# Seven block products for half of three output projections, in a two-stack transformer kernel on one core

## The reference

```python
def mamba2_mixer(h, in_w, conv_w, conv_b, dt_bias, a_log, d_skip, norm_w, out_w):
    ...
    y = y.reshape(bsz, seq, M_D_INNER).astype(h.dtype) * jax.nn.silu(z)
    gs = M_D_INNER // M_GROUPS
    y = rmsnorm_2(y.reshape(bsz, seq, M_GROUPS, gs), norm_w.reshape(M_GROUPS, gs))
    return y.reshape(bsz, seq, M_D_INNER) @ out_w

def gated_deltanet_mixer(h, in_w, conv_w, a_log, dt_bias, norm_w, out_w):
    ...
    o = rmsnorm_2(o.astype(h.dtype), norm_w) * jax.nn.silu(z.reshape(bsz, seq, G_V_HEADS, G_HEAD_DIM))
    return o.reshape(bsz, seq, G_VAL_DIM) @ out_w
```

## Time and profile before

| | before |
|---|---|
| median of three runs | 3557.66 us |
| profiled execution | 3557.7 us |
| its span, first to last instruction | 3556.0 us |
| TensorE busy | 3522.7 us, 99% |
| VectorE busy | 1956.5 us, 55% |
| ScalarE busy | 757.6 us, 21% |
| mean granted TensorE clock | 0.997 |

### The profile page before, as it was taken

The page is one execution under the profiler, slowest core; times in us unless marked ns, Lnnn a source line. Parts: engine busy times, 40 slices in busy tenths (PEclk is TensorE's granted clock), DMA queues, the critical chain, the costliest instruction groups (busy, mean ns, idle before and its releaser), DMA issues.

```text
span 3556.0 us, 47847 instructions
## 1 busy us (share of the span) xinstructions
PE 3522.7 (99%) x20724; PEld 2721.1 (77%) x20724; DVE 1956.5 (55%) x3405; ACT 757.6 (21%) x1504; POOL 52.6 (1%) x72
## 2 busy tenths in 40 slices
PE   8999999999999999999999999999999999999999
PEld 7956597794669687488868879687677968758794
DVE  6854378584535536236735648547443853635484
ACT  2003400100420045212113111042311103521110
POOL 1000000000000000000002000000000000000000
PEclk9999999999999999999999999999999999999999
DMA  9763468654325453334443434433143444334342
GB/s 414 305 263 139 169 257 330 271 208 166 119 108 190 166 190 119 130 142 160 173 166 119 179 119 167 166 140 121 72 159 127 166 166 176 147 127 151 139 166 107
DMA packets 45778, 613.32 MB, mean 172 GB/s; under 512 B 5040, under 2 KB 5056, under 8 KB 8960
## 3 DMA queue, kind: packets, MB, share of 16 engines
q1 hardware_dynamic: 41296, 590.99, 44.4%
q0 software_dynamic: 4272, 19.27, 1.4%
HBM read 607.02 MB, written 3.22 MB: 172 GB/s over the span
## 4 chain that ended last, share of the span: by engine, by line
PE 97%; ACT 1%; DVE 1%; issue 0%; DMA 0%; ACTq 0%
PE ps L3051 14%; PE ps L1513 13%; PE ps L588 9%; PE ps L481 8%; PE ps L705 7%; PE ps L567 5%; PE ps L2859 4%; PE ps L2378 4%; PE ps L2411 3%; PE ps L929 3%; PE ps L2951 3%; PE ps L1895 2%; PE ps L1915 2%; PE ps L1890 2%; PE ps L730 2%; PE ps L3245 1%
## 5 line engine op out<-in xcount | busy, mean ns | idle before, releaser
L588 PE MATMUL ps<-ring,aT 128*128 128x512 f32 x784 | 341.4, 592 | 0.0
L588 PEld LDWEIGHTS ps<-ring,aT 128*128 128x128 f32 x784 | 147.9, 190 | 179.1 <-issue 178.9
L705 PEld LDWEIGHTS ps<-hT,ring 128*128 128x128 f32 x2368 | 266.9, 192 | 5.7 <-issue 4.3
L705 PE MATMUL ps<-hT,ring 128*128 128x128 f32 x2368 | 268.4, 275 | 0.0
L567 PE MATMUL ps<-ring,aT 128*128 128x512 f32 x448 | 194.1, 592 | 0.0
L624 ACT ACTIVATE big<-x 128x1024 f32<-128x1024 f32 x34 | 35.9, 1057 | 695.2 <-DVE x L678 394.1
L2378 PE MATMUL ps<-hT,ring 128*128 128x256 f32 x768 | 173.4, 386 | 0.0
L567 PEld LDWEIGHTS ps<-ring,aT 128*128 128x128 f32 x448 | 84.5, 190 | 103.5 <-issue 103.3
L2378 PEld LDWEIGHTS ps<-hT,ring 128*128 128x128 f32 x768 | 147.7, 194 | 20.1
L3051 PE MATMUL ps<-big 128*128 128x128 f32 x1280 | 156.0, 275 | 0.0
L3051 PE MATMUL ps<-big,ring 128*128 128x128 f32 x1280 | 156.0, 275 | 0.0
(11 more groups left out here) (657 smaller groups left out, 6017.9 us busy)
## 6 DMA issues: line engine op xcount, KB each, us to landing
ring<-weights_in SPq DMA_DIRECT2D x244, 2048.0 KB, 7.8
big<-ada_in SPq DMA_DIRECT2D x36, 2048.0 KB, 9.1
aT<-rows_spill POOLq DMA_DIRECT2D x4, 1024.0 KB, 6.6
big<-rows_spill POOLq DMA_DIRECT2D x4, 1024.0 KB, 13.4
memT<-spill POOLq DMA_DIRECT2D x2, 1024.0 KB, 7.5
big<-b_gate_in POOLq DMA_DIRECT2D x1, 1536.0 KB, 18.7
aT<-mem_in SPq DMA_DIRECT2D x1, 1024.0 KB, 4.9
x<-x_in SPq DMA_DIRECT2D x1, 1024.0 KB, 12.3
```

The costliest lines, as they stand in the source:

```text
L588: last = pe.matmul(ps[:, 2 * t + half, :], aT[:, 4 * c + k, t * P:(t + 1) * P], w[:, k, half * 512:(half + 1) * 512], start=first, stop=(4 ...
L705: last = pe.matmul(ps[:, bank + m // 2, (m % 2) * SEQ + at:(m % 2) * SEQ + at + n], w[:, k, m * P:(m + 1) * P], hT[:, k, at:at + n], start ...
```

## The change

- Chunks 0 and 1 of the three projections go by seven products: 14 multiplications a chunk in place of 16 (`out_seven_pe`). Products 0, 2 and 1 come first (banks 0, 2 and 1), then 4, 5, 6 and 7 (banks 4 to 7). Before product 4 of chunk 0, TensorE now waits for the takes of quarter 2 by both engines (`base + 3`), since that quarter was turned into banks 4 and 5; before product 6 it waits for `free`, an event after which banks 6 and 7 are unused.
- Quarter 3 is turned in two halves of four transposes, both into bank 3: the first behind chunk 0, taken by VectorE, the second behind two products of chunk 1 and VectorE's take of the first, taken by ScalarE.
- VectorE makes the sums: four of 128x1024 for each of the two chunks (`out_right_dve`, each waiting for the one before it), and two sets of four of 128x256 (`out_left_dve`). In the state space mixers the first four stand behind take 0, the left sets behind gate 2 and behind take 1, the last four between gate 3 and norm 3. In the delta mixer one of the first four stands before the loop over the quarters and one behind each of the quarters 0 to 2, both left sets behind takes 0 and 1 (so before quarter 3), and the last four behind take 2.
- VectorE adds banks 4 to 7 to `x` in seven operations behind chunk 1 (`out_add_dve`), before `cross_left_dve`. The scaling of the memory for the keys (line 648) now waits for ScalarE's take of quarter 3.
- Counts of `mix_turned`, `mix_parts` and `mix_blocks` are moved accordingly in other places (GpSimd's load of the keys waits for five turns, not four).

The core of the diff:

```diff
+OUT_SEVEN = (6, 12, 15)
...
+        def out_right_dve(dve, i, c0, j, step):
+            w = arrived(dve, c0 + j).rearrange("p (q e c) -> p q e c", q=2, e=2)
...
+            if step:
+                dve.wait_ge(mix_parts, at + step)
+            if step == 0:
+                dve.tensor_tensor(t1, b12, b11, ALU.subtract).then_inc(mix_parts, 1)
+            elif step == 1:
+                dve.tensor_tensor(t2, b22, t1, ALU.subtract).then_inc(mix_parts, 1)
+            elif step == 2:
+                dve.tensor_tensor(t4, b21, t2, ALU.subtract).then_inc(mix_parts, 1)
+            else:
+                dve.tensor_tensor(b12, b22, b12, ALU.subtract).then_inc(mix_parts, 1)
...
+        def out_seven_pe(pe, i, c0, j, base, turn, n, free):
...
+            product(0, lambda q: aT[:, 2 * q + 1, 0:P], w[:, :, 1, 0:512])
+            pe.wait_ge(mix_parts, at + 12 * j + 3)
+            product(2, lambda q: aT[:, 2 * q + 1, P:SEQ], t4)
+            if j:
+                turn(pe, n, 3, 1)
+            pe.wait_ge(mix_parts, at + 8 + 4 * j)
+            product(1, lambda q: s4[:, q, :], w[:, :, 1, 512:D])
+            if j == 0:
+                pe.wait_ge(mix_act_done, base + 3)
+                pe.wait_ge(mix_dve_done, base + 3)
+            product(4, lambda q: aT[:, 2 * q, 0:P], w[:, :, 0, 0:512])
+            product(5, lambda q: s1[:, q, :], t1)
+            if j == 0:
+                pe.wait_ge(*free)
+            product(6, lambda q: s2[:, q, :], t2)
+            pe.wait_ge(mix_parts, at + 12 * j + 4)
+            product(7, lambda q: aT[:, 2 * q, P:SEQ], w[:, :, 0, 512:D]).then_inc(chunks_used, 1)
+            if j == 0:
+                turn(pe, n, 3, 0)
...
         def down_pe(pe, i, before, c0, nk, ada=(), kc0=None, ki=0, late=None, then=None, seven=None, taken=None):
...
+                if late:
+                    out_seven_pe(pe, i, c0, j, base, turn, n, free)
                     continue
...
-                if late and j == 0:
-                    turn(pe, n, 3)
...
+            if i in OUT_SEVEN:
+                out_add_dve(dve, i, c0)
+                dve.wait_ge(mix_blocks, out_adds_before(i) + 7)
...
+            out_right_dve(dve, 12, 174, 0, 0)
             for q in range(4):
...
+                if q < 3:
+                    out_right_dve(dve, 12, 174, 0, q + 1)
                 if q == 2:
                     gdn_take_dve(dve, 0)
                     gdn_take_dve(dve, 1)
+                    out_left_dve(dve, 12, 0, 4)
+                    out_left_dve(dve, 12, 1, 4)
             gdn_take_dve(dve, 2)
+            for step in range(4):
+                out_right_dve(dve, 12, 174, 1, step)
             gdn_take_dve(dve, 3)
...
             mamba_take_dve(dve, n, 0, nw_col)
+            for step in range(4):
+                out_right_dve(dve, o, c_out, 0, step)
             mamba_gate_dve(dve, n, 2)
+            out_left_dve(dve, o, 0, 8 * n)
             mamba_norm_dve(dve, n, 2)
             mamba_take_dve(dve, n, 1, nw_col)
+            out_left_dve(dve, o, 1, 8 * n)
             mamba_gate_dve(dve, n, 3)
+            for step in range(4):
+                out_right_dve(dve, o, c_out, 1, step)
             mamba_norm_dve(dve, n, 3)
             mamba_take_dve(dve, n, 2, nw_col)
             mamba_take_dve(dve, n, 3, nw_col)
```

More of the change, by code:

```diff
@@ L540, in seven_gated_add_dve, with out_sums_before, out_adds_before, out_left_part @@
             dve.tensor_tensor(x[:, 1, :], x[:, 1, :], sums[:, 1, :], ALU.add).then_inc(seven_tokens, 1)
+        MIX_SUMS, MIX_ADDS = 2 * sum(MIX_CHUNKS) + 4 * len(MIX_CHUNKS), 4 * sum(MIX_CHUNKS)
+        def out_sums_before(i):
+            return 16 * sum(1 for o in OUT_SEVEN if o < i) + (MIX_SUMS if i > 8 else 0)
+        def out_adds_before(i):
+            return 7 * sum(1 for o in OUT_SEVEN if o < i) + (MIX_ADDS if i > 8 else 0)
+        def out_left_part(i, part):
+            return view(big, 8192 + 512 * part, 4, P) if i == 12 else view(aTf, 4096 + 512 * part, 4, P)
@@ new lines, in out_left_dve @@
+        def out_left_dve(dve, i, g, base):
+            q = slice(2 * g, 2 * g + 2)
+            rows = aT[:, 0:16, :].rearrange("p (q e) c -> p q e c", e=2)
+            a11, a12, a21, a22 = rows[:, q, 0, 0:P], rows[:, q, 1, 0:P], rows[:, q, 0, P:SEQ], rows[:, q, 1, P:SEQ]
+            s1, s2, s4 = (out_left_part(i, part)[:, q, :] for part in range(3))
+            at = out_sums_before(i) + 4 + 4 * g
+            dve.wait_ge(mix_act_done, base + g + 1)
+            dve.wait_ge(mix_dve_done, base + g + 1)
+            dve.tensor_tensor(s1, a21, a22, ALU.add).then_inc(mix_parts, 1)
+            dve.wait_ge(mix_parts, at + 1)
+            dve.tensor_tensor(s2, s1, a11, ALU.subtract).then_inc(mix_parts, 1)
+            dve.tensor_tensor(a21, a11, a21, ALU.subtract).then_inc(mix_parts, 1)
+            dve.wait_ge(mix_parts, at + 2)
+            dve.tensor_tensor(s4, a12, s2, ALU.subtract).then_inc(mix_parts, 1)
@@ new lines, in out_seven_pe, with product @@
+        def out_seven_pe(pe, i, c0, j, base, turn, n, free):
+            at = out_sums_before(i)
+            w = arrived(pe, c0 + j).rearrange("p (q e c) -> p q e c", q=2, e=2)
+            t1, t2, t4 = (out_right_part(i, j, part) for part in range(3))
+            s1, s2, s4 = (out_left_part(i, part) for part in range(3))
+            def product(bank, left, right):
+                for q in range(2):
+                    last = pe.matmul(ps[:, bank, :], left(2 * j + q), right[:, q, :], start=(j == 0 and q == 0), stop=(j == 1 and q == 1), skip_group_check=True)
+                return last
+            product(0, lambda q: aT[:, 2 * q + 1, 0:P], w[:, :, 1, 0:512])
+            pe.wait_ge(mix_parts, at + 12 * j + 3)
+            product(2, lambda q: aT[:, 2 * q + 1, P:SEQ], t4)
+            if j:
+                turn(pe, n, 3, 1)
[13 more added lines that the diff above has]
+                turn(pe, n, 3, 0)
@@ new lines, in out_add_dve @@
+        def out_add_dve(dve, i, c0):
+            part, both = gdn_work[:, 0:512], gdn_work[:, 512:D]
+            at = out_adds_before(i)
+            dve.wait_ge(chunks_used, c0 + 2)
+            dve.tensor_tensor(x[:, 0, 0:512], x[:, 0, 0:512], ps[:, 4, :], ALU.add).then_inc(mix_blocks, 1)
+            dve.tensor_copy(part, ps[:, 4, :]).then_inc(mix_blocks, 1)
+            dve.wait_ge(mix_blocks, at + 2)
+            dve.tensor_tensor(part, part, ps[:, 6, :], ALU.add).then_inc(mix_blocks, 1)
+            dve.wait_ge(mix_blocks, at + 3)
+            dve.tensor_tensor(x[:, 0, 512:D], x[:, 0, 512:D], part, ALU.add).then_inc(mix_blocks, 1)
+            dve.tensor_tensor(both, part, ps[:, 7, :], ALU.add).then_inc(mix_blocks, 1)
+            dve.wait_ge(mix_blocks, at + 5)
+            half = x[:, 1, :].rearrange("p (h c) -> p h c", h=2)
+            dve.tensor_tensor(half, half, both.unsqueeze(1).to_broadcast([P, 2, 512]), ALU.add).then_inc(mix_blocks, 1)
+            dve.wait_ge(mix_blocks, at + 6)
+            dve.tensor_tensor(x[:, :, 512:D], x[:, :, 512:D], ps[:, 5, :].unsqueeze(1).to_broadcast([P, TT, 512]), ALU.add).then_inc(mix_blocks, 1)
@@ L545, in down_pe @@
             if late:
-                turn, n, base = late
+                turn, n, base, free = late
                 pe.wait_ge(mix_act_done, base + 2)
@@ L586, in down_pe @@
                         for half in range(2):
-                            first = 4 * c + k == 0 if seven is None else (t, half, c, k) == (1, 1, nc - 2, 0)
+                            first = 4 * c + k == 0 if seven is None and not late else (t, half, c, k) == (1, 1, nc - 2, 0)
                             last = pe.matmul(ps[:, 2 * t + half, :], aT[:, 4 * c + k, t * P:(t + 1) * P],
-                                             w[:, k, half * 512:(half + 1) * 512], start=first, stop=(4 * c + k == nk - 1), skip_group_check=seven is not None)
+                                             w[:, k, half * 512:(half + 1) * 512], start=first, stop=(4 * c + k == nk - 1), skip_group_check=seven is not None or late is not None)
                     if t == 1:
@@ L1003, in gdn_pe, with gdn_turn_pe @@
                 gdn_turn_pe(pe, 0, q)
-        def gdn_turn_pe(pe, n, q):
+        def gdn_turn_pe(pe, n, q, half=None):
             pe.wait_ge(mix_normed, 4 + q + 1)
-            for m in range(4):
+            if half == 1:
+                pe.wait_ge(mix_dve_done, 8)
+            for m in range(4) if half is None else range(2 * half, 2 * half + 2):
                 for t in range(TT):
                     at = (m % 2) * SEQ + t * P
-                    last = pe.transpose(ps[:, 2 * q + m // 2, at:at + P], view(big, 8192 + 1536 * q, TT, 4, P)[:, t, m, :], ident[:, :])
+                    last = pe.transpose(ps[:, 2 * q + m // 2 if half is None else 3, at:at + P], view(big, 8192 + 1536 * q, TT, 4, P)[:, t, m, :], ident[:, :])
             last.then_inc(mix_turned, 1)
@@ L2335, in mamba_y_pe, with mamba_turn_pe @@
             last.then_inc(mamba_y, 1)
```

(10 more changed lines are left out.)

51 lines of the change are left out of this document (31 added, 20 removed).

## The result

The changed kernel took 3563.56 us (median of 18 runs, 3557.3 to 3568.3), the kernel before 3557.85 us in its 18 runs (3553.68 to 3559.99). The ratio over all runs is 1.0014, with a 95% interval of 1.0008 to 1.0021; that of the two medians is 1.0016. So the kernel is slower by about 0.15%, clear of zero but under the 0.2% that the prediction set as its bound. The forecast was 3562.0 us and no change. Twelve multiplications less on the engine that is busy in 99% of the span have made the kernel slower by 5.7 us, from median to median.

What follows compares the result with a forecast made beforehand. TensorE, busy in 99% of the span, was taken to bound the kernel. 3557.7 + 0.7 (steps) + 3.6 (clock) = 3562.0 us, called no change at 0.81; range 3556 to 3566 us.

Steps and rivals of the forecast that it cites:

- The saving: Two multiplications fewer in each of two chunks at three places: 10.3 us, 3.43 us a place.
- The wait at i=6 and 15: State space mixers, TensorE before product 4 waiting for quarter 2's takes: 3.67 us lost against 3.43 saved, +0.24 a place.
- the sign: New TensorE waits on VectorE's take of quarter 2: 3.5 to 3.8 us at i=6 and 15, 3.2 to 3.5 at i=12.
- The wait at i=12: Delta mixer, same wait: 0.32 us delay before chunk 0 plus 3.34 us lost, 3.43 saved, +0.23 us.
- The cover: VectorE's adds, 13.6 us at i=12 and 15, fit before the residual add at 13.94 us: 0 us, at most 1 a place.
- The sum of the steps: Savings and waits at the three places together: 0.24 + 0.23 + 0.24 = +0.7 us.
- The clock: TensorE's clock halves for one stretch at each of the three new waits: 1.2 us a place, +3.6 us.
- The rule that was weighed: Clock swings when cycling banks: all 28 multiplications of a place at half clock, 24 us a place, 72 in all; not used.
- rival (c): Clock swings through the 28 multiplications at each place: 3630 us; chance 0.01.
- (a): At the three places the new wait costs nothing and all 10.3 us are gained: 3547.4 us; chance 0.06.
- (b): Clock falls for two stretches behind each of the three waits, 10.2 us: 3568.6 us; chance 0.11.
- (d): TensorE's products are not fewer, only reordered: 10.3 us above the forecast, 3572.3 us; chance 0.01.

Runs made afterwards that it cites:

- the kernel without the wait: Changed kernel with TensorE's products that need no bank of the takes moved ahead of the wait: 3547.98 us, ratio 0.9971 to the kernel before.
- the fill: Changed kernel plus four multiplications with overwritten result before the wait for quarter 2's takes at each of three places: 3559.23 us, ratio 1.0002 to before.

## Why the prediction was right

**The saving.** Right, and shown: 3.44 us at i=6 in the kernel without the wait, 10.0 us in all for 10.3.

**The wait at i=6 and 15.** Right in mechanism, 0.2 us short. Forecast: take 2 ends at T+8.68, TensorE resumes at T+8.82, 0.24 us more a place. Measured: T+8.87, T+9.01, 0.50 us more. The term that was mis-sized is the distance of two sums that wait for each other: 1.33 us here (1463.99 to 1465.32), where the earlier trace rows had 1.26. In both the second sum waits for the first. In the new code it also waits for the weight chunk each time (`arrived` stands inside `out_right_dve`), which the sums of the earlier trace rows do once for all four; whether this second wait makes the 0.07 us, three times a place, was not tried. The rest is the first product after the wait, 1.79 us for 1.72. In the brackets of the trace the wait is 3.7 us, within the 3.5 to 3.8 that were named as the sign.

**The wait at i=12.** The sum came out (0.27 us for 0.23), but from two terms that were off against each other, which is luck. The delay in front of chunk 0 was forecast at 0.32 us and is 0.49: from the row of line 1105 (990 before) to chunk 0 are 21.01 us for 20.52. The wait itself was forecast at 3.34 us from the end of product 1 to product 4 and is 2574.58 - 2571.38 = 3.20 us. The bracket of 3.04 us lies under the 3.2 to 3.5 that were named as the sign.

**The cover.** Right: the residual add came 2609.94 - 2596.01 = 13.93 us behind chunk 2, to the 13.94 of the earlier trace rows, with 0.57 us to spare for 0.3 forecast.

**The sum of the steps.** Forecast +0.7 us, measured +1.3 us by the places in the trace after (without the low stretch at i=12), and +1.2 us by the kernel in which work stands in place of the idle time.

**The clock.** Forecast +3.6 us from falls behind the three waits. Measured are 4.3 us as the difference between the changed kernel and the filled one, and 4.4 us as what the 5.7 leave beside the 1.3. A fall costs what was said, 1.66 us of at most 1.7. But the 1.2 us a place were argued from a fall behind every wait, a little shortened, and that is not what the traces show: one of the three waits had a fall in the trace after, and over all traces 4 of the 7 waits of 3.0 to 3.7 us and 2 of the 6 of 2.0 us. By 4 of 7 times 1.66 us the three places would cost 2.8 us, an estimate from few waits. That the sum fits is in part luck. The runs spread as falls that come only sometimes would have it: 11.0 us from lowest to highest after (18 runs), 6.3 us before (18), 2.9 us with the fill (11). The granted clock in the stretch behind a wait is shown; that it accounts for the whole 4.3 us is inferred from the fill, whose edit does nothing but put work into the idle time. One execution of each kernel was traced, and low stretches away from the three places come and go between them (five before, three after, four with the fill, where one that lasted 6.8 us is counted as two), so how many falls a median run has is not shown.

**The forecast as a whole.** 3563.56 us lies 1.6 us above the 3562.0: 0.6 from the waits, 0.8 from the clock, and 0.2 because the median of before in these runs is 3557.85 us and not the 3557.7 that the forecast began from.

**The rule that was weighed.** The swing of the clock that the Trainium skill ("TensorE: Matmul & The Clock Gate", the section on PSUM queue depth cycling) tells of for a kernel that goes through banks did not come here, and with it rival (c) fell. The products follow each other here without idle time in brackets but for the one wait. The rows decide: behind two of the three waits the granted clock was 1.00 while the products went to banks 4 to 7, and at i=12 it was half for one stretch of 3.4 us.

**The rivals.** The wait that does not bite (a) fell with the first row of the waits. The kernel with another order shows what it would have given: 3548 us, for 3547.4 forecast. Two low stretches a place (b) did not come in any trace: the second row behind the wait at i=12 is back at its own pace. It was not out of the question, since two low stretches in a row do stand elsewhere (1287.7 to 1294.6 in the trace with the fill). The products are fewer, by 3.44 us at i=6 in the kernel with the other order, so (d) fell too.

## What to carry to other kernels

Fewer instructions on the busiest engine are worth nothing where its new order asks for a buffer sooner than the slower engine frees it: add up when each engine comes to its wait before the count of what was saved. If a wait can't be made shorter, look for work that does not need it and put that in front; here the same products in another order turned 5.7 us lost into 10 us gained. And an idle stretch of TensorE has to be priced above its length, since the clock may fall behind it.

## What was not expected of the hardware

Work whose result is thrown away made a kernel faster: 12 multiplications, 10.3 us of TensorE's time, put in three idle stretches of together 10.4 us, gave 4.3 us back.

Whether the clock falls behind a wait is not settled by the wait's length alone. Behind the wait of 2.7 us at the old place in the state space mixers half the clock was granted both times in all nine traces, while of the seven waits of 3.0 to 3.7 us in the traces only four had it. What makes the difference was not tried and stays open.

A low clock also comes where TensorE has not waited at all. In the trace before, the stretches at 1287.8 and 2335.7 stand behind 32 records with only 32 columns each, with no idle time in front of them:

```profile
1284.92 4.10 PE L2355 MATMUL ps<-small,hT 128*128 128x32 f32 x32
...
2332.36 3.69 PE L913 MATMUL ps<-small,hT 128*128 128x32 f32 x32
```

Those at 1287.8 and 2987.6 were missing in the trace after, in a part of the program that the change doesn't touch. Whoever compares two single traces of such kernels has to count the low stretches first.
